# Scattering each expert's result rows to their tokens, and reading them back in order

## The reference, cut to what matters

```python
D_MODEL = 1024; N_EXPERTS = 32; TOP_K = 2; D_EXPERT = 256
g_idx = jnp.argmax(g_prob, axis=-1)                                # 1 of 4 expert groups
top_p, top_i = lax.top_k(jax.nn.softmax(e_sel, axis=-1), TOP_K)    # 2 of its 8 experts
wts = top_p / jnp.sum(top_p, axis=-1, keepdims=True) * g_top[:, None]
hg = jnp.einsum('td,edf->tef', t, w_gate)
hu = jnp.einsum('td,edf->tef', t, w_up)
hid = jax.nn.silu(hg) * hu * gates[:, :, None]
out = jnp.einsum('tef,efd->td', hid, w_down)
```

## Time and profile before

| | |
|---|---|
| median of 3 runs | 2067.32 us (2059.81 to 2068.58) |
| the profiled execution, its own time | 2069.1 us |
| its span, first to last instruction | 2067.3 us |
| busy | PE 1548.3 us (75%), DVE 700.6 (34%), ACT 462.4 (22%), POOL 235.4 (11%) |
| expert stage of layer 0 | from the first gather at 1082.65 us to the last `ex_yo` copy, which ends at 1354.68 us |
| expert stage of layer 1 | up to the last `ex_yo` copy at 1999.95 us |

### The profile page before, as it was taken

The page is one execution under the profiler, slowest core; times in us unless marked ns, Lnnn a source line. Parts: engine busy times, 40 slices in busy tenths (PEclk is TensorE's granted clock), DMA queues, the critical chain, the costliest instruction groups (busy, mean ns, idle before and its releaser), DMA issues. The chain is left out here.

```text
span 2067.3 us, 25979 instructions
## 1 busy us (share of the span) xinstructions
PE 1548.3 (75%) x10406; PEld 1131.7 (55%) x10406; DVE 700.6 (34%) x1222; ACT 462.4 (22%) x775; POOL 235.4 (11%) x310
## 2 busy tenths in 40 slices
PE   2599899965499879849549978832996936988852
PEld 0599644431199768449526544522996924544431
DVE  1422254442315473461351111126235253111106
ACT  1322255531114231121120101013223130101102
POOL 1000022210000063310001101021002001111110
PEclk9799899987599696579769999965998967999985
DMA  6032476649422210402357999931232183999962
GB/s 250 21 97 76 187 298 212 216 160 379 160 81 82 87 81 11 159 5 82 127 226 299 384 390 398 395 117 42 81 100 66 42 349 122 384 388 397 394 241 102
DMA packets 129459, 397.40 MB, mean 192 GB/s; under 512 B 15810, under 2 KB 63554, under 8 KB 106562
## 3 DMA queue, kind: packets, MB, share of 16 engines
q1 hardware_dynamic: 110242, 356.78, 45.9%
q10 hardware_dynamic: 11488, 21.24, 2.8%
q0 software_dynamic: 7616, 17.84, 2.7%
HBM read 366.49 MB, written 37.19 MB: 195 GB/s over the span
## 5 line engine op out<-in xcount | busy, mean ns | idle before, releaser
L2208 PE MATMUL ex_gups<-ex_gu,ex_he 128*64 128x256 f32 x2048 | 253.0, 403 | 63.2 <-DMA ex_gu<-in_moe_w_up 60.0
L2208 PEld LDWEIGHTS ex_gups<-ex_gu,ex_he 128*64 128x64 f32 x2048 | 151.2, 145 | 146.6 <-DMA ex_gu<-in_moe_w_up 67.6
L224 PE MATMUL sc_ps<-h_hi,sc_hi 128*128 128x272 f32 x384 | 111.3, 290 | 20.7 <-PEq L1749 20.7
L2253 DVE TENSOR_TENSOR ex_hid<-ex_sg,ex_gups 128x128 f32<-128x128 f32 x64 | 18.4, 288 | 314.8 <-ACT ex_sg L2277 314.8
L2226 PE MATMUL ex_yps<-ex_dn,ex_hid_t 128*64 128x512 f32 x512 | 123.9, 604 | 0.9 <-issue 0.9
L2186 POOL DMA_INDIRECT ex_hg<-h_rows,route_tok x64 | 60.3, 942 | 517.8 <-PE ex_trps L2198 431.6
L224 PE MATMUL sc_ps<-h_hi,sc_w_r 128*128 128x272 f32 x384 | 111.0, 289 | 0.0
L224 PE MATMUL sc_ps<-hT_r,sc_hi 128*128 128x272 f32 x384 | 110.9, 289 | 0.0
L224 PE MATMUL xbcz_ps<-mixT_r,xbcz_hi 128*128 128x272 f32 x320 | 93.4, 292 | 16.2 <-DVE xbcz_w_r L321 16.2
L224 PE MATMUL xbcz_ps<-mixT_r,xbcz_w_r 128*128 128x272 f32 x320 | 93.1, 291 | 0.0
L224 PE MATMUL xbcz_ps<-hT_r,xbcz_hi 128*128 128x272 f32 x320 | 93.0, 291 | 0.0
(11 more groups left out here) (416 smaller groups left out, 3442.0 us busy)
## 6 DMA issues: line engine op xcount, KB each, us to landing
ex_gu<-in_moe_w_gate SPq DMA_DIRECT2D x64, 1024.0 KB, 24.2
ex_gu<-in_moe_w_up SPq DMA_DIRECT2D x64, 1024.0 KB, 26.0
ex_dn<-in_moe_w_down SPq DMA_DIRECT2D x64, 1024.0 KB, 25.9
ada_rest_w<-in_ada_w SPq DMA_DIRECT2D x40, 1024.0 KB, 4.9
as_pages<-in_cache_kT SPq DMA_DIRECT2D x32, 512.0 KB, 6.3
as_pages<-in_cache_v SPq DMA_DIRECT2D x32, 512.0 KB, 5.2
y_rows<-ex_yo ACTq DMA_DIRECT2D x128, 128.0 KB, 7.0
qkv_w<-in_mix_w_in SPq DMA_DIRECT2D x12, 1024.0 KB, 5.1
```

The lines of the kernel that those rows point to most:

```text
L224: last = nc.tensor.matmul(ps[:, h, 0:HALF], w[:, j, f], x(j)[:, cols], start=(j == 0 and n == 0), stop=(j == kt - 1 and n == 2))
L2208: last = nc.tensor.matmul(gu_ps[64 * q:64 * q + 64, :, :], he[n % 2][:, j, :], ex.gu[n % S][:, :, j, q * P:(q + 1) * P], start=(j == 0), s ...
L2253: nc.vector.tensor_tensor(hid[:, :], sg[:, :], gu_ps[:, 1, :], ALU.mult).then_inc(done["hid"], 1)
```

## The change

An indirect DMA on POOL now writes each expert's results. Partition p of `ex_yo` goes to row `route_dst[p, n]` of `y_rows`, which is reshaped to 2176 rows of 512 values: row 2 x (choice x 544 + token) + half. Empty places have a number out of range and are skipped. So `y_rows` is in the order of the tokens, and `phase_combine` reads it with ten direct DMAs on SP. ACT's two direct DMAs per expert are gone, and so are `route_slot` and the clearing of `y_rows` in `phase_ssd`. The routing phase makes `route_dst` beside `route_tok`: `row_hot` is 128 wide instead of 64, `sl_ps` has 128 partitions, the number in `blk_hot` tells the choice as well, two small DVE steps are gone and four are new. POOL's order in the expert stage is: gather n, then scatter n-4; the last four scatters follow at the end, and POOL waits for all of them. The second pass is changed alike.

```diff
...
@@ -1289,17 +1288,12 @@
...
                 sp.dma_start(sst[:, :, :], io["ssm_state"]).then_inc(s["sload"], 16)
-
-                sp.wait_ge(s["zeroed"], 1)
-                for i in range(NE * CAP, NBLK * CAP, P):
-                    sp.dma_start(k.y_rows[i:i + P, :], zero_rows).then_inc(s["cleared"], 16)
                 sp.wait_ge(s["st"], 4)
...
                 sp.wait_ge(s["sst"], 16 * (1 + NB))
-                sp.wait_ge(s["cleared"], 16 * (OVB * CAP // P))
@@ -1586,7 +1580,6 @@
...
             def _(pool):
-                nc.gpsimd.memset(zero_rows, 0.0).then_inc(s["zeroed"], 1)
                 own = Chain(pool, s["own_p"])
...
@@ -1870,8 +1863,9 @@
...
         block_id = sb("block_id", [P, NBLK])
-        row_id = sb("row_id", [P, CAP])
-        tok_id = sb("tok_id", [P, TT])
+        row_id = sb("row_id", [P, 2 * CAP])
+        pair_id = sb("pair_id", [P, 2, TT])
+        half = sb("half", [P, 1])
         full = sb("full", [P, MAXQ])
@@ -1887,15 +1881,16 @@
...
         blk, row, rk, q_, ov = (sb(n, [P, 2, TT]) for n in ("blk", "row", "rk", "q", "ov"))
-        row_hot = sb("row_hot", [P, 2, CAP])
+        row_hot = sb("row_hot", [P, 2, 2 * CAP])
         blk_hot = sb("blk_hot", [P, 2, NBLK])
-        slot_f = sb("slot_f", [CAP, NBLK])
-        none = sb("none", [CAP, NBLK])
+        slot_f = sb("slot_f", [P, NBLK])
+        none = sb("none", [P, NBLK])
+        dst_f = sb("dst_f", [P, NBLK])
         tr_ps = [k.ps(f"{nm}tr{i}", [P, 512], ctx) for i in range(2)]
...
         rk_ps = k.ps(nm + "rkps", [P, TT + 1, NE], ctx)
-        sl_ps = k.ps(nm + "slps", [CAP, NBLK], ctx)
+        sl_ps = k.ps(nm + "slps", [P, NBLK], ctx)
@@ -1905,10 +1900,13 @@
...
                 own.did(nc.gpsimd.iota(block_id[:, :], [[1, NBLK]], base=0, channel_multiplier=0, **kw))
-                own.did(nc.gpsimd.iota(row_id[:, :], [[1, CAP]], base=0, channel_multiplier=0, **kw))
-                own.did(nc.gpsimd.iota(tok_id[:, :], [[P, TT]], base=1, channel_multiplier=1, **kw))
+                own.did(nc.gpsimd.iota(row_id[:, :], [[0, 2], [1, CAP]], base=0, channel_multiplier=0, **kw))
+                own.did(nc.gpsimd.iota(pair_id[:, :, :], [[T, 2], [P, TT]], base=1, channel_multiplier=1, **kw))
+                own.did(nc.gpsimd.memset(half[:, :], 1.0))
                 own.did(nc.gpsimd.iota(full[:, :], [[CAP, MAXQ]], base=CAP, channel_multiplier=0, **kw))
                 own.step(nc.gpsimd.memset(valid[:, :], 1.0))
+                own.did(nc.gpsimd.affine_select(out=half[:, :], in_=half[:, :], pattern=[[0, 1]], base=-CAP,
+                                                channel_multiplier=1, compare_op=ALU.is_ge, fill=0.0))
                 own.step(nc.gpsimd.affine_select(out=valid[:, :], in_=valid[:, :], pattern=[[-P, TT]], base=T - 1,
@@ -2094,23 +2092,25 @@
...
                 step(V.tensor_tensor(blk[:, :, :], blk[:, :, :], ov[:, :, :], ALU.add))
-                step(V.scalar_tensor_tensor(out=rk[:, :, :], in0=blk[:, :, :], scalar=float(CAP), in1=row[:, :, :],
-                                            op0=ALU.mult, op1=ALU.add))
-                step(V.tensor_copy(r.slot[:, :, :], rk[:, :, :]))
                 for n in range(2 * TT):
...
                     own.settle()
-                    V.tensor_scalar(blk_hot[:, i, :], block_id[:, :], blk[:, i, t:t + 1], tok_id[:, t:t + 1],
+                    V.tensor_scalar(blk_hot[:, i, :], block_id[:, :], blk[:, i, t:t + 1], pair_id[:, i, t:t + 1],
                                     ALU.is_equal, ALU.mult).then_inc(s["pair"], 1)
...
                                             op0=ALU.add, op1=ALU.add))
-                step(V.tensor_copy(r.tok[:, :], slot_f[:, :]))
+                own.did(V.tensor_scalar(none[:, :], slot_f[:, :], float(T), -float(T), ALU.is_ge, ALU.mult))
+                own.did(V.tensor_scalar(dst_f[:, :], slot_f[:, :], 2.0, half[:, 0:1], ALU.mult, ALU.add))
+                own.settle()
+                own.did(V.tensor_copy(r.dst[:, :], dst_f[:, :]))
+                own.step(V.tensor_tensor(slot_f[:, :], slot_f[:, :], none[:, :], ALU.add))
+                step(V.tensor_copy(r.tok[:, :], slot_f[0:CAP, :]))
@@ -2179,6 +2179,13 @@
...
+        def put_rows(pool, n):
+            pool.wait_ge(done["yo"], n + 1)
+            nc.gpsimd.indirect_dma_start(out=k.y_rows,
+                                         out_offset=bass.IndirectOffsetOnAxis(ap=r.dst[:, n:n + 1], axis=0),
+                                         in_=yo[n % 2][:, :], in_offset=None, bounds_check=4 * T - 1,
+                                         oob_is_err=False).then_inc(put[n % 2], 16)
+
         def pool_main(pool):
@@ -2186,6 +2193,12 @@
...
                                              bounds_check=T - 1, oob_is_err=False).then_inc(got[n % 2], 16)
+                if n >= 4:
+                    put_rows(pool, n - 4)
+            for n in range(NE - 4, NE):
+                put_rows(pool, n)
+            for p in range(2):
+                pool.wait_ge(put[p], 16 * (NE // 2))
@@ -2263,12 +2276,8 @@
...
                 if n >= 2:
-                    act.wait_ge(put[p], 32 * (n // 2))
+                    act.wait_ge(put[p], 16 * (n // 2))
                 nc.scalar.activation(yo[p][:, :], y_ps[p][:, :], ACT.Copy).then_inc(done["yo"], 1)
-                act.wait_ge(done["yo"], n + 1)
-                for c in range(2):
-                    act.dma_start(k.y_rows[n * CAP:(n + 1) * CAP, c * 512:(c + 1) * 512], yo[p][64 * c:64 * c + 64, :])\
-                       .then_inc(put[p], 16)
@@ -2278,8 +2287,7 @@
...
             keep_result(NE - 1)
-            for p in range(2):
-                act.wait_ge(put[p], 32 * (NE // 2))
+            act.wait_ge(done["yo"], NE)
...
@@ -2439,21 +2458,17 @@
...
     gathered = [k.sem(f"{nm}gathered{t}") for t in range(TT)]
+    by_token = k.y_rows.rearrange("(r c) f -> r (c f)", c=2)
     with ExitStack() as ctx:
...
         with nc.Block() as block:
-            @block.gpsimd
-            def _(pool):
+            @block.sync
+            def _(sp):
                 for t, (a, m) in enumerate(TOK):
                     for i in range(2):
-                        nc.gpsimd.indirect_dma_start(out=y[0:m, t, i, :], out_offset=None, in_=k.y_rows,
-                                                     in_offset=bass.IndirectOffsetOnAxis(ap=r.slot[0:m, i, t:t + 1],
-                                                                                         axis=0),
-                                                     bounds_check=NBLK * CAP - 1, oob_is_err=False).then_inc(gathered[t], 16)
-                for t in range(TT):
-                    pool.wait_ge(gathered[t], 32)
+                        sp.dma_start(y[0:m, t, i, :], by_token[i * T + a:i * T + a + m, :]).then_inc(gathered[t], 16)
@@ -2507,7 +2522,7 @@
...
         k.h_rows = nc.dram_tensor("h_rows", (T, D), F32).ap()
-        k.y_rows = nc.dram_tensor("y_rows", (NBLK * CAP, D), F32).ap()
+        k.y_rows = nc.dram_tensor("y_rows", (4 * T, D // 2), F32).ap()
         k.cT = k.sb("cT_sb", [P, KT, 32])
```

More of the change, by code:

```diff
@@ L2289, in block_programs @@
             st = [k.sem(f"{nm}{pass_name}st{b}") for b in range(2)]
+            yo_free = [k.sem(f"{nm}{pass_name}yo_free{b}") for b in range(2)]
             def sync_program(sp):
@@ L2298, in sync_program, with put_more @@
                             load_slot(sp, b, i * MORE + (MORE + b))
+            def put_more(pool, n):
+                pool.wait_ge(sems["yo"], n + 2)
+                nc.gpsimd.indirect_dma_start(out=k.y_rows,
+                                             out_offset=bass.IndirectOffsetOnAxis(
+                                                 ap=r.dst[:, first + n:first + n + 1], axis=0),
+                                             in_=yo[n % 2][:, :], in_offset=None, bounds_check=4 * T - 1,
+                                             oob_is_err=False).then_inc(st[n % 2], 16)
+                pool.wait_ge(st[n % 2], 16 * (n // 2 + 1))
+                pool.sem_inc(yo_free[n % 2], 1)
             def pool_program(pool):
@@ L2309, in pool_program @@
                                                  bounds_check=T - 1, oob_is_err=False).then_inc(g[n % 2], 16)
+                    if n >= 2:
+                        put_more(pool, n - 2)
+                for n in range(MORE * rounds - 2, MORE * rounds):
+                    put_more(pool, n)
             def tensor_program(pe):
@@ L2360, in scalar_program @@
                         act.wait_ge(sems["y"], i * MORE + (b + 1))
-                        act.wait_ge(st[p], i * (16 * MORE) + 32 * (b // 2 + 1))
+                        act.wait_ge(yo_free[p], i * (MORE // 2) + (b // 2 + 1))
                         nc.scalar.activation(yo[p][:, :], y_ps[p][:, :], ACT.Copy).then_inc(sems["yo"], 1)
-                        act.wait_ge(sems["yo"], i * MORE + (b + 2))
-                        for n in range(2):
```

(4 more changed lines are left out.)

7 lines of the change are left out of this document (3 added, 4 removed).

## The result

The kernel after the change takes 2074.38 us (median of 8 runs, 2070.07 to 2079.80) against 2067.56 us before on the same chip (8 runs). The ratio is 1.0038 (95% interval 1.0022 to 1.0055): about 7.9 us slower by the ratio and 6.8 by the medians, where 2059 us, some 8 us faster, was forecast.

The account below looks back on a forecast made before the run. DMA engine time in the weight stream was taken as the bound. Per layer -5.5 + 1.2 + 1.2 - 1.3 = -4.4, two layers -8.8: 2060.3, less 1.8 for the median, rounded to 2059; own range 2053 to 2064, wider 2048 to 2070.

Parts of the forecast that it names:

- POOL, ACT and SP in the stream: 0: Expert stage: a second indirect issue per expert fits on POOL, and ACT's saved issues gain nothing; 0 us.
- part 4: Stage end: the last result write lands at 1358.8 instead of 1357.6; +1.2 us per layer (+0.3 to +2.4).
- part 1: Expert weight stream: scatters move only filled rows, freeing DMA engine time; -5.5 us per layer, 1 under the even 6.5.
- price by bytes alone: Expert stream: a scatter costs only its bytes, 6.4 engine-us, saving 9.1 us per layer; as rival 2051, chance 0.15.
- term for unevenness: Expert stream: allowance for engines not ending together, 1 us per layer off the even saving.
- Uneven engines: Expert stream: a scatter's fixed partition sets give one engine places nearly always filled, shrinking the saving; chance 0.20.
- mild form: Expert stream: four low and four high places per engine, saving 3.3 us per layer; 2063, chance 0.15.
- hard form: Expert stream: eight neighbouring places per engine, nothing saved, seams' +1.1 left, up to +5.7; 2070 to 2079, chance 0.05.
- part 2: Routing before the expert stage: wider one-hot rounds and four more small steps, two gone; +1.2 us per layer (0.5 to 2.0).
- part 5: Combining: direct SP reads bring the first data sooner, -1.3 us per layer (-2.2 to 0); later groups gain nothing.
- part 6: Clearing of y_rows dropped: eight SP issues and 4 MB of traffic go; cost and gain 0.
- late-scatter rival: Expert stream: scatters land too late for ACT's copies, deciding only beyond 16.7 us; about 2150 at 20; chance 0.05.

Follow-up runs that it names:

- late gather: Kernel before the change, with one more unused token gather on POOL after the last result copy of each expert stage: 2073.63 us, ratio 1.0039.
- drain in mid-stage: Changed kernel, with an explicit drain on POOL ahead of its last four scatters: 2062.60 us, ratio 0.9979.
- control: Kernel before the change (direct result writes), with each token's place turned by 10 per expert block: 2072.08 us, ratio 1.0029.
- other places: Changed kernel, with four neighbouring partitions taking places 16 apart (only the pattern of row_id differs): 2077.83 us, ratio 1.0059.
- late scatters: Changed kernel, with the last two scatters moved past the block's end, to the start of POOL's next block: 2059.56 us, ratio 0.9972.
- turned places: The late scatters kernel, with each token's place turned by 10 per expert block, modulo 64: 2056.33 us, ratio 0.9947.
- direct reads: Kernel before the change, with the combining's ten indirect gathers replaced by ten direct reads on SP, rows not the tokens': 2063.54 us.
- no writes: Kernel before the change, with y_rows cleared first and only the last two experts' results written: 2034.81 us.
- turn 2: The turned places kernel, with a turn of 2 places per block in place of 10: 2056.87 us, ratio 0.9951.

## Why the prediction was wrong

It had two main faults, one in a term it never wrote down, one in a term whose condition it named and didn't believe.

**The seam (parts 3, 4 and 5; forecast -0.1, measured +5.5 and +3.7).** The failing step is "POOL, ACT and SP in the stream: 0", together with part 4, which ended the last write at its landing and let all that follows stay as it was. From the copy's end to the first read's issue the kernels have 9.27 and 9.20 us before and 14.39 and 13.75 after. In these +5.1 and +4.6, the scatter adds 0.2 and POOL's DRAIN, now on the path, 5.29 us. Off come 0.5 and 0.7 us, as SP issues its first read sooner after PE's branch than POOL did, and in layer 1 another 0.5, as that branch was shorter. The prediction asked what a second indirect transfer costs POOL in the stream, and found cover for it; it didn't ask what POOL does between its last transfer and the block's end, and what had covered that. A gap between the last landing (1357.6) and the first gather (1363.95) was in the earlier trace rows for it to see, but the DRAIN before lay elsewhere. The late gather, the drain in mid-stage and the moved scatters show the cause from three sides. In the forecast's terms this puts its 0 at +5.3 us per layer; it is the larger part of a miss of 8 us per layer.

**The stream (part 1; forecast -5.5, measured -2.6 and -2.5).** The step that failed is "I take 5.5 us per layer, 1 us under the even value", with the unevenness put at 1 us. The traffic fell by more than was forecast. From 1105 to 1345 us, q0 took 10.2% of 16 x 240 = 392 engine-us for 28 gathers and scatters, 14.0 for a pair against 7.8 + 11.4 = 19.2 before: 5.2 saved per expert, where 3.6 was forecast: the price by bytes alone, the lower one, was the better (an empty place cost a packet of 9 to 13 ns, not 32, and 4096 bytes 205 ns in a gather before, 185 after). The engines' mean followed: weights every 8.90 us instead of 9.23. What PE saw of it was 2.6, and in layer 1 perhaps less. So the term for unevenness, put at 1 us, was in truth some 5 us or more per layer (an estimate: 0.33 us for each of 24 experts in those 220 us is 8, less 2.6). Where the engines are even, a saving of 4.4 and 5.9 us arrives against a control that has even engines too, but evening itself made the packets dearer. So the runs show that unevenness hid the saving, by the taper and by the mean, and not that it could all have been had. In the changed kernel the intervals stay at 9.09 and the gain shows as a taper. That is the rival *Uneven engines*, in its mild form as a size (2 to 3 us gained per layer), by its hard form as a mechanism in the bound part, where nothing is gained. The reasoning against it took the shortness of the taper before as a proof of even dealing. But there the results were written in direct transfers of all 64 rows, nothing of them skipped, so the taper before spoke of the gathers alone; and dealing in turn over the engines was not among the cases weighed. The prediction's own signs for this (a share under 1 while PE waits, an interval of 9.1) were both met.

**Routing (part 2; +1.2).** From the first one-hot operation to the first gate and up product it was 15.90 and 15.72 us and is 17.84 and 18.06; less 0.41 for the two small steps that went: +1.5 and +1.9, inside 0.5 to 2.0 though above the +1.2. The steps, in time:

```profile
1065.73 0.29 DVE L2099 TENSOR_SCALAR rt_row_hot<-rt_row_id,rt_row 128x128 f32<-128x128 f32 x1
...
1067.12 0.29 DVE L2099 TENSOR_SCALAR rt_row_hot<-rt_row_id,rt_row 128x128 f32<-128x128 f32 x1 [0.22 <-PE rt_slps L1956]
...
1073.68 0.19 DVE L2108 TENSOR_SCALAR rt_none<-rt_slot_f 128x48 f32<-128x48 f32 x1
1073.79 0.24 DVE L2109 TENSOR_SCALAR rt_dst_f<-rt_slot_f,rt_half 128x48 f32<-128x48 f32 x1
1074.06 0.19 DVE L2111 CAST route_dst<-rt_dst_f 128x48 int32<-128x48 f32 x1
1074.16 0.20 DVE L2112 TENSOR_TENSOR rt_slot_f<-rt_slot_f,rt_none 128x48 f32<-128x48 f32 x1
```

Two pairs took 1.39 us instead of 1.14: twice 0.04 for the width, and 0.22 of waiting for PE's product, so 0.12 per round (1.39 - 1.14 over two) where the forecast took 0.08 out of 0.03 to 0.13. Over ten rounds, +1.3. The rest of the table's difference lies ahead of the rounds, 1.0 us shorter in layer 0 and 0.5 longer in layer 1.

**The last write (part 4; +1.2).** The issue followed the copy by 0.77 us and landed 2.4 later: 3.2 us, against 2.9 before. So +0.2 to +0.3, the term's lower bound. The gathers' 3.0 was the wrong row for a write. (The term's upper bound, +2.4, would be +3.0 by its own figures: 1354.68 + 0.9 + 5 is 1360.6.)

**The combining (part 5; -1.3).** -1.4 and -1.3 when done alone, with the luck told above; inside the changed kernel +0.4 and -0.9 from the first read's issue to the scaling. From the first scaling to the residual phase nothing changed (22.54 and 22.56 us).

**Clearing (part 6) and the other rivals.** From the first `dA` of the scan phase to SP's first load of `out_w`, just ahead of the next norm, it was 154.1 us before and 152.3 after. But without clearing it was 154.4, 154.8, 154.7 and 154.6 in the kernels with a drain in mid-stage, other places, late scatters and turned places, and with it 153.9 and 151.5 with the late gather and the direct reads. No gain is to be seen, as forecast. The scatters landed in 7.3 us where the late-scatter rival needed 16.7, and forecast 11.5. Empty places were skipped: q0 moved 8.10 MB, filled rows alone.

## What to carry to other kernels

When a transfer is moved to the end of a block, look at what its engine does after it and when it did so before: an engine that had finished early was paying for things out of sight. On POOL that is 0.083 us for each indirect transfer since its last drain, with quiet queues; drain it once while others still work, or leave the last few transfers to the next block. And where many DMA engines share a stream, a saving counts for the slowest of them alone: check how rows are dealt, look for a lengthening taper rather than at the mean share, and compare the mean rate of delivery with the interval of the engine that waits.

## What the runs showed of the hardware

POOL's DRAIN at a block's end grows with the indirect transfers it has issued, 5.29 us for 64 and 2.75 for 33, also when all of them have long landed. Where it began with the last issue still running and the stream at its full rate, it took 8.5 to 10.6 us for 32 to 60 of them; in the fading stream 6.3 to 6.9 for 62.

The rows of an indirect write of 128 partitions are dealt to the DMA engines in pairs of neighbours, as far as the runs tell in turn. The pairs stand in the sizes of the packets (4096, 2052 and 8 bytes). The turn is inferred from one other order of places, which left a share of 0.51 as if half of the engines had ended, and from the taper that went away when places were turned.

A weight packet of 8192 bytes is not of fixed price: 332 ns before, 334 after, 340 without the writes, 339 in the turned kernel before, 344 to 349 with scatters and turned places, at a mean share of 1.02 in all. A saving in engine-us was therefore worth 87% of its sixteenth part even where it was the same on all engines.

PE's branch into the block after the experts took 3.0 to 4.0 us in 19 of the 24 layers traced and 0.44 or 0.45 us in five. The traces tell them apart. In all 19 a packet of 16384 bytes on queue q8, whose kind is `instruction`, started 0.6 to 1.6 us after the branch did. In the five none ran during the branch, and one had started 6.8 to 9.7 us ahead of it. The five lie all in layer 1 (late gather, drain in mid-stage, late scatters, no writes, turn 2), so seams of single profiles differ by 3 us for this alone.
